# A norm's row factor moved from the input of a projection to its outputs, in a one-core float32 block

## The reference, cut to what matters

```
n  = x * rsqrt(mean(x*x, axis=-1) + EPS) * g_mix        # rms_norm, one factor per token
z  = n @ w_in + b_in
q, k, v, u, bg, cg, ga, gc = split(z)                   # 512 x6, 1024, 1024 columns
ya = attention(rms_norm(q, g_q), rms_norm(k, g_k), v)   # 8 heads of 64, norms per head
yc = bg * causal_conv3(cg * u)
m  = sigmoid(ga) * (ya @ w_pa) + sigmoid(gc) * (yc @ w_pc)
h  = x + m @ w_o
```

## Time and profile before

| | us |
|---|---|
| median of 3 runs | 1940.49 (1937.89 to 1942.53) |
| the profiled execution | 1941.41 |
| its span | 1939.2 |
| PE busy | 1879.0 (97%) |
| DVE busy | 918.7 (47%) |
| ACT busy | 637.6 (33%) |
| POOL busy | 139.6 (7%) |

### The profile page before, as it was taken

The page is one execution under the profiler, slowest core; times in us unless marked ns, Lnnn a source line. Parts: engine busy times, 40 slices in busy tenths (PEclk is TensorE's granted clock), DMA queues, the critical chain, the costliest instruction groups (busy, mean ns, idle before and its releaser), DMA issues.

```text
span 1939.2 us, 31375 instructions
## 1 busy us (share of the span) xinstructions
PE 1879.0 (97%) x13564; PEld 1563.2 (81%) x13564; DVE 918.7 (47%) x1611; ACT 637.6 (33%) x1187; POOL 139.6 (7%) x120
## 2 busy tenths in 40 slices
PE   7999999999999989999899999999999999999998
PEld 6877788866666666669789999999867898888898
DVE  5766334233333333348873422347767574423345
ACT  6344323121111011126432222234466543222242
POOL 0022000110000000000000000004222100000001
PEclk9999999999999999999899999999999999999999
DMA  5222342689999999973112232234321213232343
GB/s 191 88 76 77 97 167 92 270 349 429 428 430 429 427 429 429 427 282 99 56 45 88 88 107 79 88 109 142 109 66 55 79 54 109 89 109 85 101 127 121
DMA packets 57149, 345.16 MB, mean 178 GB/s; under 512 B 7168, under 2 KB 7808, under 8 KB 44976
## 3 DMA queue, kind: packets, MB, share of 16 engines
q1 hardware_dynamic: 53184, 334.15, 46.3%
q0 software_dynamic: 3504, 8.54, 1.3%
q10 hardware_dynamic: 320, 0.43, 0.1%
HBM read 343.09 MB, written 4.19 MB: 179 GB/s over the span
## 4 chain that ended last, share of the span: by engine, by line
PE 82%; DVE 8%; DMA 6%; ACT 1%; issue 1%; POOL 1%; DVEq 0%; SPq 0%; ACTq 0%; POOLq 0%
PE bank L499 56%; PE bank L714 9%; DMA e<-in_we 6%; PE bank L738 5%; PE bank L555 1%; PE bank L749 1%; PE bank L750 1%; DVE wlo L1331 1%; PE bank L1147 1%; PE bank L1095 1%; PE bank L892 1%; PE bank L701 1%; PE bank L1067 1%; PE bank L931 1%; PE bank L572 1%
## 5 line engine op out<-in xcount | busy, mean ns | idle before, releaser
L1331 DVE TENSOR_TENSOR wlo<-raw,whi 128x1024 fp32r<-128x1024 f32 x230 | 288.3, 1260 | 127.2 <-ACT whi L2332 123.4
L2332 ACT CAST whi<-raw 128x1024 fp32r<-128x1024 f32 x231 | 239.9, 1043 | 122.8 <-PE bank L499 105.6
L714 PE MATMUL bank<-e,xT 128*64 128x256 f32 x2048 | 234.7, 382 | 1.3 <-DVE xT L1604 1.0
L714 PEld LDWEIGHTS bank<-e,xT 128*64 128x64 f32 x2048 | 143.2, 137 | 80.6 <-issue 12.5
L499 PE MATMUL bank<-nhi,whi 128*128 128x272 f32 (+1 forms) x672 | 191.7, 285 | 1.1 <-DVE sl L1860 0.6
L499 PE MATMUL bank<-nhi,wlo 128*128 128x272 f32 (+1 forms) x672 | 191.3, 285 | 0.0
L499 PE MATMUL bank<-nlo,whi 128*128 128x272 f32 (+1 forms) x672 | 190.7, 284 | 0.0
L499 PE MATMUL bank<-n1hi,whi 128*128 128x512 f32 (+1 forms) x448 | 162.7, 363 | 0.0
L499 PE MATMUL bank<-n1lo,whi 128*128 128x512 f32 (+1 forms) x448 | 160.8, 359 | 0.0
L499 PE MATMUL bank<-n1hi,wlo 128*128 128x512 f32 (+1 forms) x448 | 160.7, 359 | 0.0
L499 PEld LDWEIGHTS bank<-nhi,whi 128*128 128x128 f32 x672 | 127.2, 189 | 2.0 <-DVE sl L1860 0.8
(11 more groups left out here) (405 smaller groups left out, 3762.4 us busy)
## 6 DMA issues: line engine op xcount, KB each, us to landing
e<-in_we SPq DMA_DIRECT2D x94, 2048.0 KB, 21.8
raw<-in_w_down SPq DMA_DIRECT2D x64, 512.0 KB, 3.6
raw<-in_w_gate SPq DMA_DIRECT2D x44, 512.0 KB, 3.5
raw<-in_w_up SPq DMA_DIRECT2D x44, 512.0 KB, 3.5
raw<-in_w_q SPq DMA_DIRECT2D x12, 512.0 KB, 4.5
B<-in_rel POOLq DMA_DIRECT2D x8, 512.0 KB, 4.7
raw<-in_w_gc SPq DMA_DIRECT2D x8, 512.0 KB, 3.6
raw<-in_w_ga SPq DMA_DIRECT2D x8, 512.0 KB, 4.3
```

The costliest lines, as they stand in the source:

```text
L714: p = e.matmul(b[64 * hf:64 * hf + 64, 0:256], x[:, k, :], W[:, k, 256 * hf:256 * hf + 256], start=(k == 0), stop=(k == 7))
L1331: e.tensor_tensor(wlo[wslot(u)][:], raw[u % NRAW][:], whi[wslot(u)][:].bitcast(F32), ALU.subtract).then_inc(*hit("dve_low", ("lo", u)))
L2332: e.copy(whi[wslot(u)][:], raw[u % NRAW][:]).then_inc(*hit("act_high", ("hi", u)))
```

## The change

`x` is turned once, unscaled, straight out of `xt`. `xhi` and `xlo` are made of the unscaled x, and the same banks are copied to `hT` (DVE copies blocks 1 to 3, ACT block 0 and 4 to 7), which now frees the bank in place of the making of `xlo`; `pe_raw_x` and the scaled `xr` are gone. The root of each token is still made by DVE. It is put on a diagonal (`dg`), multiplied by ones on PE in 16 pieces of 32 columns (`pe_spread_x`, each a plain float32 matmul), so that every partition has the 512 factors, and copied by ACT to `rb`. DVE multiplies each q, k, cg, u, bg, gc and ga product by `rb` (`x_scaled`, or `x_scaled_there` in place in the bank), ACT then works on the result in SBUF. The values take the factor as the scalar of the eviction that they have anyway. Eight `hsq` buffers stand in place of two. Weight unit 0 is loaded ahead of x. The ticks ahead of the side work are counted anew, `HEAD_LAG` is 5 and then 6.

```diff
         def pe_load():
             for i in range(4):
-                w.wait_ge(*at("xr", i))
+                w.wait_ge(*at("x", i))
-                    p = e.transpose(bank[BANK["x", k]][:, i * 128:(i + 1) * 128], xr[:, i, k * 128:(k + 1) * 128], ident)
+                    p = e.transpose(bank[BANK["x", k]][:, i * 128:(i + 1) * 128], xt[:, i, k * 128:(k + 1) * 128], ident)
-        def pe_raw_x(ks):
...
+        def pe_spread_x():
+            b = take(("rb x",), SIDE)
+            w.wait_ge(*at("diag x"))
+            for i in range(4):
+                for c in range(0, 128, 32):
+                    p = e.matmul(b[:, i * 128 + c:i * 128 + c + 32], ones, dg[:, i, c:c + 32], start=True, stop=True)
+            p.then_inc(*hit("pe_norm", ("spread x",)))
+            yield
@@ tensor
-        side.add(nothing(3))
+        side.add(nothing(8))
         side.add(pe_meta())
-        side.add(pe_raw_x(range(6)))
+        side.add(nothing(2))
+        side.add(pe_spread_x())
         for i in range(8):
-            side.add(nothing(HEAD_LAG))
+            side.add(nothing(HEAD_LAG[i]))
             side.add(pe_head_norm(i))
-            if i == 2:
-                side.add(pe_raw_x((6, 7)))
-    HEAD_LAG = 2
+    HEAD_LAG = (5,) + 7 * (6,)
@@ vector, dve_load
             feed(0)
+            root_x(0)
             for k in range(8):
                 w.wait_ge(*at("x hi", k))
                 e.scalar_tensor_tensor(xlo[:, k, :], bk("x", k), v1("g_mix", k), xhi[:, k, :].bitcast(F32), ALU.mult,
-                                       ALU.subtract).then_inc(*hit("dve_norm", ("xn", k), ("free", "x", k)))
+                                       ALU.subtract).then_inc(*hit("dve_norm", ("xn", k)))
+            for k in (1, 2, 3):
+                e.tensor_copy(hT[:, k, MT:L], bk("x", k)).then_inc(*hit("dve_out", ("free", "x", k)))
+            root_x(2)
+            e.tensor_tensor(dg[:], ident.unsqueeze(1).to_broadcast([128, 4, 128]),
+                            xs[:, 0, 0:4].unsqueeze(2).to_broadcast([128, 4, 128]), ALU.mult).then_inc(
+                                *hit("dve_norm", ("diag x",)))
+        def x_scaled(to, *key):
+            w.wait_ge(*at("free", "rb x"))
+            w.wait_ge(*at("out", *key))
+            e.tensor_tensor(to, bk(*key, 0), rb[:, 0:S], ALU.mult).then_inc(*hit("dve_out", ("free", *key, 0)))
@@ vector
-        side.add(nothing(3))
+        side.add(nothing(8))
         side.add(dve_meta())
-        side.add(nothing(14))
+        side.add(nothing(9))
         for i in range(8):
             tile(J["q" if i < 4 else "k"], i % 4)
-            side.add(nothing(HEAD_LAG))
+            for j in (0, 1) if i == 1 else (i,) if i else ():
+                dve_head(j)
+            side.add(nothing(HEAD_LAG[i]))
             side.add(dve_head_norm(i))
-            if i == 2:
-                side.add(nothing(4))
@@ vector, dve_conv
                 tile(J["cg", i], 0, at_k={CONV_LAG: lambda: conv_low(i - 1)} if i else {})
-                tile(J["u", i], 0)
+                tile(J["u", i], 0, at_k={1: factor})
+                x_scaled_there("u", i)
...
                 tile(J["bg", i], 0, at_k={1: first, 3: lambda: tap(1), 5: lambda: tap(2)})
+                x_scaled_there("bg", i)
@@ scalar, act_load
+            feed(0)
+            for i in range(3):
+                x_square(i)
+            w.wait_ge(*at("vec"))
+            x_high(0)
+            x_high(1)
+            x_copy(0)
+            x_high(2)
+            x_high(3)
+            feed(1)
+            for k in range(4, 8):
+                x_high(k)
+            x_square(3)
+            for k in range(4, 8):
+                x_copy(k)
@@ sync
+        load(0)
         for i in range(4):
             e.dma_start(xt[:, i, :], T["x"][i * 128:(i + 1) * 128, :]).then_inc(*dma(f"d_x{i}", ("x", i)))
         for u in range(U_MOE):
-            load(u)
+            if u:
+                load(u)
```

More of the change, by code:

```diff
@@ L215, in _program @@
     yclo = pl("yclo", [128, 4, S], F32R)
-    hsq = [pl(f"hsq{i}", [128, S]) for i in range(2)]
+    hsq = [Place(XR + 2048 * i)(f"hsq{i}", [128, S]) for i in range(8)]
+    pl.off += 4096
     mt_ = pl("meta", [MT, D])
@@ L536, in pe_head_norm @@
             w.wait_ge(*at("hsq", i))
-            e.matmul(b[:], half, hsq[i % 2][:], start=True, stop=True).then_inc(*hit("pe_norm", ("head sum", i)))
+            e.matmul(b[:], half, hsq[i][:], start=True, stop=True).then_inc(*hit("pe_norm", ("head sum", i)))
             yield
@@ L1466, in dve_mix, with gate @@
             for h in range(4):
-                for m in range(2):
-                    tile(J["ga", h], m)
+                def gate(m):
+                    w.wait_ge(*(at("m", 2 * h + m - 2) if h else at("yc", 3)))
+                    x_scaled(sg[:, m, :], "ga", 2 * h + m)
+                tile(J["ga", h], 0)
+                tile(J["ga", h], 1, at_k={1: lambda: gate(0)})
                 for m in range(2):
                     k = 2 * h + m
-                    tile(J["pa", h], m)
-                    w.wait_ge(*at("free", "ga", k, 0))
+                    tile(J["pa", h], m, at_k={} if m else {1: lambda: gate(1)})
+                    w.wait_ge(*at("gate a", k))
                     w.wait_ge(*at("out", "pa", k))
@@ L1487, in dve_mix @@
                 w.wait_ge(*at("out", "wo", m))
-                w.wait_ge(*at("free", "raw x", m))
+                w.wait_ge(*at("free", "x", m))
                 e.tensor_tensor(hT[:, m, MT:L], hT[:, m, MT:L], bk("wo", m, 0), ALU.add).then_inc(
@@ L2433, in act_branches, with gate @@
                     tile(J["gc", h], m, at_k={CONV_LAG - 1: lambda: conv_high(3)} if k == 0 else {})
[L2434 to L2437 removed]
+                    if m:
+                        gate(k - 1)
                 for m in range(2):
                     tile(J["pc", h], m)
+                    if m == 0:
+                        gate(k)
             side.drain()
[L2442 to L2447 removed]
         def act_mix():
+            def gate(k):
+                z = sg[:, k % 2, :]
+                w.wait_ge(*at("free", "ga", k, 0))
+                e.activation(z, z, ACT.Sigmoid, bias=v1("b_in", 24 + k)).then_inc(*hit("act_out", ("gate a", k)))
             for h in range(4):
@@ L2453, in act_mix @@
                     tile(J["ga", h], m)
-                    w.wait_ge(*at("out", "ga", k))
-                    if h:
-                        w.wait_ge(*at("m", k - 2))
-                    else:
-                        w.wait_ge(*at("yc", 3))
-                    e.activation(sg[:, m, :], bk("ga", k, 0), ACT.Sigmoid, bias=v1("b_in", 24 + k)).then_inc(
-                        *hit("act_out", ("free", "ga", k, 0)))
+                    if m:
+                        gate(k - 1)
                 for m in range(2):
@@ L2942, in scalar @@
         act_load()
-        side.add(nothing(4))
-        side.add(act_raw_x(range(6)))
-        side.add(nothing(1))
+        side.add(nothing(13))
         for i in range(8):
             tile(J["q" if i < 4 else "k"], i % 4)
-            act_head(i)
-            side.add(nothing(HEAD_LAG))
+            if i == 1:
+                w.wait_ge(*at("spread x"))
+                e.copy(rb[:, 0:S], bk("rb x")).then_inc(*hit("act_out", ("free", "rb x")))
+            for j in (0, 1) if i == 1 else (i,) if i else ():
+                act_head(j)
+            side.add(nothing(HEAD_LAG[i]))
             side.add(act_head_norm(i))
-            if i == 2:
-                side.add(act_raw_x((6, 7)))
         act_values()
@@ L3107, in low @@
                 *hit("pool_low", ("lo", u)))
-        low(1)
+        for u in POOL_LOW:
+            low(u)
         pool_attention()
```

112 lines of the change are left out of this document (53 added, 59 removed).

## The result

The changed kernel took 1946.73 us in the median (1944.69 to 1951.44, 9 runs) beside 1940.49 for the kernel before, timed with it: a ratio of 1.0034, 95% interval 1.0025 to 1.0042. It is slower, by 0.34%; the forecast was 1941.5 with 1945.2 as its upper end. The profiled execution has a span of 1944.9, 5.7 more than before.

What follows compares the result with a forecast made beforehand. PE, busy 97% of the span, was taken as the bound. Terms -4.6 - 2.6 + 0.6 + 3.2 + 3.6 + 0.6 + 0.2 = +1.0 us on the median 1940.49 gave 1941.5, range 1937.2 to 1945.2.

Steps and rivals of the forecast that it cites:

- t: First tile: moment ACT makes xhi 0, forecast 11.3 us against 15.33 before, bounds 11.0 and 12.0.
- 0.175 each: Start: price per turning of x on PE, from 32 turnings in 5.61 us.
- if the turnings are slower in the beginning: Start: upper bound for the first xhi, 12.0 us, since the turning rate used is an average.
- Rival (d): First tile: PE's clock is low, eight triples at half speed, about 4 us more, 1945.5; chance 0.05.
- Raw x, meta, and the spread: PE's own work: -2.6 for turning raw x, +0.6 for the meta turning, +3.2 for 32 spread records.
- A clock of 0.5 after it: Sign that the forecast is wrong: PE's clock at 0.5 after the spread; no cost given.
- Tick 73 against 72: DVE: head norm 7 falls behind the last value eviction, adding 4.05 us ahead of attention unit 0; PE waits +3.6.
- Rival (a): Head-norm tail: hidden ahead of the last value eviction or by slack at unit 0; -2.6, 1937.9; chance 0.14.
- rival (b): Attention unit 0: PE's clock falls to half in the new wait, losing 1.6 us, 1943.1; chance 0.12.
- Unit 11: Convolution: bg's multiply of 0.68 on DVE delays this attention unit, slack 0.06, PE waits +0.6.
- Rival (c): Convolution: slower in-place multiplies on DVE, or POOL slowed beside them, six narrow units pay; +4.0 more, 1945.5; chance 0.08.
- The multiply frees it within 1: Gates: gc 1's bank, wanted 2.7 us after filling, is freed within 1; no cost, at most 0.7 at four places.

Runs made afterwards that it cites:

- filled_unit_0: Changed kernel plus 7 plain 256-column matmuls, results unread, ahead of the turning of attention unit 0: 1948.54 us, ratio 1.0033 to the kernel before.
- best16_filled_unit_15: Changed kernel with grouped 14-piece spread, head norms one tick earlier, later yalo, two early matmuls, plus 4 unread 256-column matmuls at attention unit 15: 1938.39 us, ratio 0.9987.

## Why the prediction was wrong

**The start: mechanism right, size off.** The steps behind t held: first dense matmul at t + 2.15 (12.58 + 2.15 = 14.73), the diagonal in time, the spread after the counted ticks. t itself was 12.58 and not 11.3, beyond even its upper bound of 12.0. The term that failed is "0.175 each": that is an average over the 32 turnings of before, which has two rates in it, 17 in 3.62 us and then 17 in 1.99 (those on the border count in both; each line has the stretch, its length, PE busy, weight loads busy, clock, DMA share, GB/s):

```profile
10.00:14.00 4.00, 3.62 (x17) 3.65 (x18) 1.00 1.03 419
14.00:16.00 2.00, 1.99 (x17) 1.75 (x15) 1.00 0.50 201
```

The 25 turnings that the first `xhi` needs lie almost wholly in the slow part here and take 5.68 us, with a pause of 0.28 for x1 in it. At 0.21 each the turnings and not x3 are what ends last, and t is 11.7 by the prediction's own start of 6.3. Another 0.5 is that start: ACT starts on x0 at 6.70 against 5.01, so it landed 1.7 us later than before and not 1.25, and PE began at 6.81. The bound "if the turnings are slower in the beginning" named this and stopped 0.6 short. How far off it is was partly the draw: with the same start, other kernels' profiles have t from 11.16 on, and t follows the moment at which PE gets to the fast rate. A slip of the prediction without consequence stands beside it: "PE waits about 1.5 us inside this tile" should be 0.8 by its own terms (8.4 - 2.15 - 5.48), and it was 0.6. Error +1.3 in t, +1.4 at the end of the tile. Rival (d) didn't come: 18 dense matmuls from 18.21 took 4.41, full speed. (Its price was too low besides: eight triples at half speed are 8 x 0.69 = 5.5 more, not 4.)

**PE's own work: right.** Raw x, meta, and the spread at 3.49 by the row of L656 (3.2 forecast). 14 pieces with the same 512 columns took 3.05, 4 pieces 0.89: the price goes by records, at the 0.11 of the turnings, which was the prediction's bound of 3.5. The floor of about 25 ns per small matmul that the Trainium skill has (page "TensorE: Matmul & The Clock Gate", section "Back-to-back issue gap") would have made 0.8 of the 16 pieces; it isn't seen here.

**The clock behind the spread: not foreseen as a cost.** "A clock of 0.5 after it" stood only among the signs of error, without a price or a chance. It costs 1.65 us in the profiled run, and the clock fell there in four of six profiles with such a spread.

**The tail of the head norms: right.** Tick 73 against 72, an inversion behind the last eviction, 3.6 us of wait: all as worked out, and one tick less takes 5.7 off the median. Rival (a) is refuted. What failed is the step after it: the clock was held to stay up because the wait is shorter than the 5.20 of the earlier trace rows, and rival (b) had 0.12. It fell, for 1.6, and in all seven profiles that have this wait unfilled there is half clock in or behind it. The evidence against that reasoning stood in the trace of before and wasn't read: 2.19 us of idle PE at unit 15 already had half clock behind it.

**Unit 11: right**, 0.56 for 0.6. Rival (c), a slower DVE in the convolution, is refuted: the multiply takes 0.68 into SBUF and 0.70 in place, and no other unit got a new wait.

**The gate multiplies: wrong.** "The multiply frees it within 1" priced the multiply and not its place in DVE's queue. DVE stood at the `yalo` tick for ACT, and the bank came 1.42 late with a `wlo` in between. The upper bound of 0.7 was too low as well, since it counted only the multiply's own time. Moving the `yalo` takes it away. It happened once, not at four places.

**The kernel before had a loss of its own** of 1.6 at unit 15, which the changed kernel escaped in its profiled run. This was luck: the same wait is in every unfilled profile, with the fall in seven of fifteen. A forecast relative to one profile carries such a draw with it.

In sum, +1.4 (start), +0.3 (spread), +1.65 and +1.6 (clock), +1.7 (gates), -0.2 (other units) and -1.6 (unit 15) make 4.85 us; the span is 4.7 above the forecast one (1944.9 against 1940.2). Two clock falls came and one went, so the clock is a third of it. The stated range also stopped at 1945.2, below the 1945.5 that (c) and (d) have in the same text. That idle time is what brings the clock down is best shown at unit 0: half clock in all seven profiles with the wait, none in the one where it is filled or in the nine without it. At unit 15 the two filled profiles have full clock, but so have eight unfilled ones, and the median's 1.2 us is not clear of noise; at unit 0 the median did not come down at all. Why the clock fell behind the spread and at unit 15 in some executions and not in others stays open, and so does the cause of the stop near 870.

## What to carry to other kernels

When an operation moves to another engine's queue, ask what that queue is waiting for at this place; here the operation's duration of 0.68 was the smaller part of its price. When ticks or slots are counted, one too many can cost a whole inversion at the end of the list, so count the last item and not the first. Price a new wait on PE with the half clock that may follow it, and look through the trace of before for the shortest wait that had one behind it. An average over a group in which the engine changes its speed is no price for the first of the group: split it first.

## What the runs showed of the hardware

**PE is slow at the start of the program, and the clock column doesn't tell.** Plain matmuls of 32 columns took 0.22 per record at 5.11 us (24 in 5.33) and 0.12 at 198.94 (20 in 2.42); turnings took 0.21 each from 6.81 to 12.3 and about 0.11 behind that. The trace's first record of the clock, full clock, begins at 12.30 in the changed kernel and at 14.34 before, just where the turnings get fast; ahead of it there is none, and the column prints 1.00 where nothing is recorded. The Trainium skill, page "TensorE: Matmul & The Clock Gate", section "The HAM clock gate", has a PE that comes from idle start at the 1.2 GHz level; the ratio of the durations agrees, and so does the place of the first record. When the clock rises differs from run to run: between 9.62 and 12.85 us in the eleven profiles with the same start. The 24 small records from 5.11 on did not bring it forward (14.06), and the 26 turnings behind them took 4.71, 0.18 each.

**The clock also fell while PE was busy without a gap**: 32 records of the spread in 3.49 us, then 0.50, in four of six profiles with such a spread. The same waits did not always do the same: 3.6 us idle had half clock in or behind it seven times of seven, 2.19 us seven times of fifteen.

**A stop of PE with no releaser**, 1.5 to 2.3 us near 870 us behind a branch, in all four kernels with 24 matmul records fewer than the changed kernel, in none of the profiles with as many or more, wherever the replacements stand, and with about 10 us of half clock behind it. Those four have 109 packets on the page's instruction queue, all kernels with the old count 108. The two with more matmuls (filled_unit_0, best16_filled_unit_15) also have 109; their profiled executions show no stop, but their times spread as widely (1942.7 to 1951.8, 1935.7 to 1942.7), so a stop in some of their executions is possible and wasn't seen. The Trainium skill, page "Runtime: NRT & Kernel Launch", section "Instruction fetch mechanics", says that instructions come in blocks and that a taken branch to a block not yet loaded stalls; that would fit, but no run here shows a fetch, so it is not shown as the cause.
